# Down weights of experts 7 to 28 asked for from the scalar engine's queue in a two-layer mixture-of-experts step

## The reference, cut to what matters

```python
def _hier_moe(x, w_coarse, b_coarse, w_fine, b_fine, w_gate_up, w_down):
    ...
    for g in range(N_GROUPS):
        gate_g = jnp.where((grp == g)[:, None], gates, 0.0).astype(x.dtype)
        hg, hu = jnp.split(jnp.einsum('nd,edf->nef', xt, w_gate_up[g]), 2, axis=-1)
        out = out + jnp.einsum('nef,efd->nd', jax.nn.silu(hg) * hu * gate_g[..., None], w_down[g])
```

## Time and profile before

| what | value |
|---|---|
| median of 3 runs | 1172.88 us (1172.82 to 1174.65) |
| the profiled execution | 1173.51 us, its span 1171.0 us |
| PE busy | 1072.5 us (92% of the span), mean granted clock 0.982 |
| DVE, ACT, POOL busy | 497.3, 230.7, 196.6 us |
| SP's queue (q1) | 279.57 MB, 60.0% of 16 DMA engines' span |
| POOL's queue (q0) | 74.01 MB, 16.1% |
| ACT's queue (q10) | 4.19 MB, 1.0% |
| L1983, gate and up products | 188.7 + 94.1 us busy |
| L2010, down products | 122.7 us busy |

### The profile page before, as it was taken

One profiled execution on the slowest core, in us unless ns is written; L12 is line 12 of the kernel. 1 busy time (PEld: TensorE's weight loads), 2 busy tenths in 40 slices (PEclk: granted clock), 3 DMA queues, 4 the chain that ended last, 5 costly groups with the idle time before them and its releaser, 6 DMA issues. The chain is left out here.

```text
span 1171.0 us, 15355 instructions
## 1 busy us (share of the span) xinstructions
PE 1072.5 (92%) x5821; PEld 539.0 (46%) x5821; DVE 497.3 (42%) x1377; ACT 230.7 (20%) x515; POOL 196.6 (17%) x190
## 2 busy tenths in 40 slices
PE   8999999999999999986999999999999999889782
PEld 6874555655543333332543446544555433333230
DVE  3713686577741221111662414564777321112126
ACT  0311233321221000100511213343212100110003
POOL 0003000000011111100546633220000121111123
PEclk9999999999999999999999999999999999999995
DMA  8421120449489999997989988893976999999976
GB/s 302 150 86 70 69 82 2 153 192 420 182 330 420 420 420 420 420 421 300 389 323 387 391 315 351 309 400 151 378 321 261 357 410 418 421 420 420 421 327 231
DMA packets 86154, 358.82 MB, mean 306 GB/s; under 512 B 13991, under 2 KB 18220, under 8 KB 56380
## 3 DMA queue, kind: packets, MB, share of 16 engines
q1 hardware_dynamic: 64188, 279.57, 60.0%
q0 software_dynamic: 19808, 74.01, 16.1%
q10 hardware_dynamic: 2080, 4.19, 1.0%
HBM read 342.75 MB, written 31.16 MB: 319 GB/s over the span
## 5 line engine op out<-in xcount | busy, mean ns | idle before, releaser
L1983 PE MATMUL ahead_psum<-m_wg,top_xT 128*64 128x512 f32 x704 | 188.7, 596 | 7.3 <-DMA m_wg<-in_moe_w_gate_up 7.3
L2010 PE MATMUL n_psum_m<-m_wd,top_xT 128*64 128x512 f32 x456 | 122.7, 608 | 12.2 <-issue 9.9
L1983 PEld LDWEIGHTS ahead_psum<-m_wg,top_xT 128*64 128x64 f32 x704 | 59.2, 137 | 97.0 <-issue 83.6
L1450 PE MATMUL ahead_psum<-top_wide,top_xT 128*128 128x512 f32 x224 | 102.1, 599 | 1.5 <-PEq L159 1.5
L1983 PE MATMUL ahead_psum<-top_wide,top_xT 128*64 128x512 f32 x288 | 94.1, 595 | 2.2 <-DMA top_wide<-in_moe_w_gate_up 1.2
L1892 POOL DMA_INDIRECT expert_rows<-e_Y,m_dest x33 | 33.2, 1007 | 352.6 <-DVE e_Y L2062 295.7
L2457 PE MATMUL ahead_psum<-top_wide,top_xT 128*128 128x512 f32 x192 | 85.4, 596 | 0.3 <-ACT top_xT L2748 0.3
L2246 POOL DMA_INDIRECT cd_kv<-in_cache_kT,top_kpages x64 | 64.0, 1000 | 44.6 <-PE cd_psum_d L2500 26.0
L2053 DVE COPY top_xT<-n_psum_t 128x512 f32<-128x512 f32 x31 | 21.4, 692 | 115.0 <-PE n_psum_t L1966 115.0
L2010 PEld LDWEIGHTS n_psum_m<-m_wd,top_xT 128*64 128x64 f32 x456 | 38.9, 140 | 65.8 <-issue 63.2
L2106 DVE TENSOR_TENSOR top_xT<-top_xT,ahead_psum 128x256 f32<-128x256 f32 x31 | 13.0, 421 | 120.2 <-ACT top_xT L2076 120.2
(11 more groups left out here) (542 smaller groups left out, 1631.5 us busy)
## 6 DMA issues: line engine op xcount, KB each, us to landing
m_wg<-in_moe_w_gate_up SPq DMA_DIRECT2D x96, 1024.0 KB, 24.1
m_wd<-in_moe_w_down SPq DMA_DIRECT2D x54, 1024.0 KB, 24.4
top_wide<-in_moe_w_gate_up SPq DMA_DIRECT2D x32, 1024.0 KB, 21.0
cd_kv<-in_cache_kT SPq DMA_DIRECT2D x64, 256.0 KB
top_X<-in_moe_w_down SPq DMA_DIRECT2D x8, 1024.0 KB, 22.1
ab_w<-in_ab_w_in SPq DMA_DIRECT2D x2, 2048.0 KB, 11.6
top_wide<-in_ab_w_in SPq DMA_DIRECT2D x2, 2048.0 KB, 7.8
top_wide<-in_ab_w_out SPq DMA_DIRECT2D x2, 2048.0 KB, 8.8
```

Of the source, the lines that this page charges most:

```text
L1450: last = nc.tensor.matmul(half_bank(i, h)[:P, :], mixT[:, k, tok0(t):tok0(t) + P], w[h][:, k, :], start=(k == 0), stop=(k == KD - 1))
L1983: last = nc.tensor.matmul(pg[i % 2][64 * a:64 * a + 64, :], xgT[i % 2][:, j, 64 * a:64 * a + 64], wg[E.slot(i, a)][:, j * 512:(j + 1) * 51 ...
L2010: last = nc.tensor.matmul(py[n2][64 * a:64 * a + 64, :], hT[:, j, 64 * a:64 * a + 64], wd[E.slot(i, a)][:, j * D + n2 * 512:j * D + (n2 + ...
```

## The change

The loop on SP no longer asks for down weights. ACT asks for them: for pair 0 between its copies for pairs 1 and 2, for pair 1 before `silu(2)`, and for pairs 2 to 10 right behind `copy_h(i)`. The call waits for `dn` as before, now on ACT. The requests themselves (size, buffers, semaphores) are the same, 22 in each layer. Groups 11 and 12 are left on SP.

```diff
@@ -1930,7 +1930,6 @@
         last = (NE - 1 - E.RING) // 2
         for p in range(last - 1):
             E.reload_up(sp, p, gh, gu)
-            E.reload_down(sp, p, dn)
         E.reload_up(sp, last - 1, gh, gu)
         E.reload_up(sp, last, gh, gu)
         if by_column_halves:
@@ -2075,6 +2074,8 @@
             act.wait_ge(hr, i)
             nc.scalar.activation(sg, pg[i % 2][:, 0:DE], ACT.Silu).then_inc(sl, 1)
 
+        on_act = range((NE - 1 - E.RING) // 2 - 1)
+
         def run(lo, hi):
             if lo > 2:
                     copy_x(lo, 0, act, xta)
@@ -2084,13 +2085,18 @@
                     copy_h(i - 1)
                 if i + 1 < hi:
                     copy_x(i + 1, 0, act, xta)
+                if i == 2:
+                    E.reload_down(act, 1, dn)
                 if i < hi:
                     silu(i)
                 if i in by_arrival:
                     copy_h(i)
+                    if i in on_act:
+                        E.reload_down(act, i, dn)
 
         copy_h(0)
         copy_x(1, 0, act, xta)
+        E.reload_down(act, 0, dn)
         copy_x(2, 0, act, xta)
         silu(1)
         run(2, main)
```

## The result

The changed kernel takes 1182.16 us (median of 11 runs, 1178.34 to 1185.54) against 1174.77 us of the kernel before in the same runs (1172.22 to 1177.04). The ratio is 1.0056, 95% interval 1.004 to 1.0071: 6.6 us slower at this size. The profiled execution took 1180.18 us with a span of 1177.6, that is 6.7 and 6.6 us over the profiled execution of before.

The account below looks back on a forecast made before the run. The prediction took the full DMA engines (420 GB/s) to bound the expert stages. Nothing gained on SP, nothing paid on ACT, 6 us lost by the order of service: 1172.9 + 6 = 1179 us, range 1173.0 to 1186.0.

Parts of the forecast that it names:

- Full DMA engines, so no gain from SP's freedom: Expert stages: DMA engines full at 419 to 421 GB/s, so taking 22 requests a layer off SP gains 0.
- ACT pays nothing: ACT behind copy_h: its wait and two requests (0.80 us) fit into its idle time, 7.7 us left; cost 0.
- A half share for ACT's queue: Expert stages: ACT's queue gets half the rate, so 2 MB of down weights land within 10 us and a bit.
- Layer 0's steps: Layer 0, pairs 11 to 15: expert 23's weights 8.8 to 11.3 us late, the layer loses 4.2 to 6.7 us.
- Layer 1: Layer 1, pairs 11 to 15: expert 23's weights land late, pair 15 comes at 1111.3 to 1113.8, 1.1 to 3.6 us lost.
- The sum: Both layers' losses together: 5.3 us with one request of group 10 ahead, 10.3 with two; 6 taken.
- nothing to be seen: Both layers: ACT's queue gets a third, later waits absorb most of the delay; 1174.6 us, chance 0.21.
- Faster: Expert stages: two queues keep the DMA engines busier by 2% or more; 1164.4 us, chance 0.09.
- ACT held: Both layers: ACT's requests blocked behind SP's full queue, 2.3 us a pair, 23 us in all; 1196 us, chance 0.05.

Follow-up runs that it names:

- groups 7 and 8: Changed kernel with ACT making only the down requests of groups 7 and 8, SP the others: 0.9998 of the kernel before.
- groups 7 to 10: Changed kernel with ACT making only the down requests of groups 7 to 10, SP those of groups 0 to 6: 1.0071 of the kernel before.
- group 10 alone: Changed kernel with ACT making only group 10's two down requests in each layer, SP the others: 1.0011 of the kernel before.
- last kernel: Kernel before with expert 28's down request moved behind all up requests in layer 0 only: 1172.44 against 1174.17 us, ratio 0.998.

## Why the prediction was right, and where it was not

- **Full DMA engines, so no gain from SP's freedom:** right. Up requests were asked for up to a few us earlier and landed later; the slices stay at 420 to 421 GB/s.
- **ACT pays nothing:** right. The two requests take 0.82 us for 0.80 forecast (one pair of layer 1 takes 1.8 us), even while a single request of SP took 4.8 us (from 450.6 us on); ACT's idle time before its copy is the same 8.31 us. The kernel with groups 0 to 6 on ACT costs nothing that can be seen.
- **A half share for ACT's queue:** nearly right, 5.6 us for the second megabyte where a half gives 5.0. But the rows that it was read from don't show it. Between 1117.5 and 1122.2 us of the kernel before the queues stand so:

```profile
q0 software_dynamic: 213, 1.60, 81.5%
q1 hardware_dynamic: 69, 0.39, 19.9%
```

POOL's queue had four fifths then and SP's one, and with 0.39 MB left for SP's queue more than half of its last megabyte had moved before 1117.5, so 4.7 us between two landings was no measure of a share. That the share came out near a half was luck in this respect. And 2 MB did not land "within 10 us and a bit" of their request but after 15.3 us. The landing times were forecast at 10 to 14 us and are 9.7 and 14.9 at group 8, median 12.4.

- **Layer 0's steps:** pair 8 begins 1.16 us earlier in this execution. With that added, pair 12 begins at 501.8 (forecast 501.2 to 503.7), pair 13 at 515.5 (514.9 to 517.4), pair 14 at 529.2 (528.6 to 531.1). The stage lost 4.3 us, forecast 4.2 to 6.7. The agreement is better than the working, which put pair 11's second half 8.8 to 11.3 us late. With the 1.16 us added it began 7.9 us late (expert 23 was put off by 11.7 us, forecast 12.5 to 15), and 1.4 us more came from the slow block behind it, a term that the sum does not have. Two mis-sized terms made up for each other: whole requests of group 10 were added, while a wait at pair 9 and its slow block, not in the steps, had put off that request to 482.8, and its first megabyte landed at 492.4, behind expert 23.
- **Layer 1:** forecast 1.1 to 3.6, measured 3.7. Pair 11's second half began 7.2 us late, within the forecast 5.7 to 8.2, and nothing made up for the clock's term: PE waited 0.72, 2.06 and 4.09 us at pairs 10 and 11, and the block behind the last took 5.16 us.
- **The sum:** 6 us forecast, 6.6 us measured by the ratio. The two stages alone lost 8.0 us; the difference to 6.6 lies within what the rest of the kernel varies by. Without the two slow blocks (1.42 and 1.51 us) the stages would have lost 5.1 us, under the lower end of the sum, 5.3: that 6 was met so closely is in part luck.
- **The rivals:** "nothing to be seen" needed 15 us for 2 MB and, in layer 0, group 10 behind expert 23, and both are there. Expert 23 landed at 491.2 us there in the time of the kernel before, between this case's 489.6 and the forecast's 492.1, and the slow block made the loss larger still. In layer 1 group 10's first megabyte landed at 1069.8 us, just ahead of expert 23 (1070.2), as in the forecast, and 3.7 us were lost where this case has none. The waits at pairs 13 to 15 alone, which it needed too, are not there. "Faster" needed more than 420 GB/s: not there. "ACT held" needed requests of several us: not there. The Trainium skill's sentence that several issuers save only the time to ask ("DMA: Bandwidth & Descriptors", "Issuing engines are not separate DMA queues") holds for the rate here, 420 GB/s in both kernels, and not for the time of the kernel, 0.56% more: the interleaving it also states is what lets the down weights overtake the up weights here.

What stays open: how much of each slow block belongs to the clock in runs that are not profiled. The lengths come from one profiled execution for each kernel, so differences of a few tenths of a us between them are not to be relied on.

## What to carry to other kernels

With the DMA engines full, the second queue here was not more bandwidth but another priority: what was put on the short queue overtook what waited in the long one (12.4 us to landing against 27.5). So don't give it what is needed last (giving it what is needed first was not tried here), and check at which point of the stage the overtaken transfers had their smallest margin; a loss well ahead of it is taken up again (groups 7 and 8), one close to it stays (groups 7 to 10). A wait of PE should be priced with the block behind it, which took 1.4 to 2.9 us more here where it was slow.

## What was not expected of the hardware

- A wait of 1.45 us was followed by a slow block (5.35 us for 3.65, group 10 alone), one of 3.15 us by none (groups 7 and 8, pair 10, layer 0), a wait of 2.74 us by none (kernel before, pair 15) and one of 2.73 us by one of 5.00 us (last kernel). The length of the wait alone does not say what follows it, and some of the spread between executions of one kernel may come from this; that was not tried.
- Up requests stood far longer in SP's queue than in the kernel before, 42.5 us for expert 23's second half and 49.8 us at most, where 32.2 us was the longest there. SP was then held for up to 7.8 us by a single request. When one of SP's took 4.8 us from 450.6 us on, ACT's two at 450.3 and 450.7 us took 0.82 together: a full queue of SP did not hold ACT's requests here.
